# Routed experts on one core: a full-rate one-hot scatter with gates per slot, a reordered expert tail, and TensorE's pair loop written out

## The reference, cut to what matters

```python
logits = h @ w_router                       # 256 x 8
top_val, top_idx = lax.top_k(logits, 2)
top_w = softmax(top_val)
gates = sum(one_hot(top_idx, 8) * top_w)    # 256 x 8, two entries per token
for e in range(8):
    y = (silu(h @ w_gate[e]) * (h @ w_up[e])) @ w_down[e]   # 1024 -> 3584 -> 1024
    out = out + gates[:, e:e+1] * y
```

## Time and profile before

| | |
|---|---|
| median of 3 runs | 1938.88 us (1936.35 to 1943.38) |
| profiled execution, time / span | 1940.5 / 1938.8 us |
| PE, DVE, ACT, POOL busy, share of the span | 95%, 71%, 59%, 51% |
| mean granted clock of TensorE | 0.969 of full |
| bytes moved by DMA | 479.5 MB |

### The profile page before, as it was taken

One profiled execution on the slowest core, in us unless ns is written; L12 is line 12 of the kernel. 1 busy time (PEld: TensorE's weight loads), 2 busy tenths in 40 slices (PEclk: granted clock), 3 DMA queues, 4 the chain that ended last, 5 costly groups with the idle time before them and its releaser, 6 DMA issues.

```text
span 1938.8 us, 26811 instructions
## 1 busy us (share of the span) xinstructions
PE 1835.8 (95%) x9778; PEld 1564.0 (81%) x9778; DVE 1374.6 (71%) x1144; ACT 1142.2 (59%) x941; POOL 982.0 (51%) x476
## 2 busy tenths in 40 slices
PE   7979999998999998999989999999999899879999
PEld 6769998887787887887878878878788697769998
DVE  6455445454788887797878877988888776367775
ACT  6434444463676776766757767767677454535553
POOL 6030000101796976978959879789597214620000
PEclk9999999998999999999999999999999898689999
DMA  6445555532898997998989989989899433215551
GB/s 202 173 134 170 180 195 174 174 109 79 325 369 305 376 366 271 378 361 310 368 300 334 365 305 378 363 307 371 302 378 367 146 109 109 87 44 174 189 181 66
DMA packets 248535, 479.53 MB, mean 247 GB/s; under 512 B 15919, under 2 KB 84297, under 8 KB 248409
## 3 DMA queue, kind: packets, MB, share of 16 engines
q1 hardware_dynamic: 247545, 476.49, 69.8%
q10 hardware_dynamic: 864, 1.31, 0.2%
HBM read 476.72 MB, written 1.05 MB: 246 GB/s over the span
## 4 chain that ended last, share of the span: by engine, by line
PE 80%; DVE 9%; issue 5%; ACT 4%; POOL 1%; DVEq 0%; DMA 0%; SPq 0%; ACTq 0%; POOLq 0%
PE bank L1881 24%; PE bank L1883 23%; PE bank L1882 23%; DVE wl L1494 3%; PE bank L2177 2%; PE bank L2254 2%; ACT wh L1026 1%; PE bank L2207 1%; PE bank L1847 1%; DVE xT L1252 1%; DVE arena L1532 1%; PE bank L2315 0%; PE bank L1967 0%; DVE wl L438 0%; POOL wl L438 0%
## 5 line engine op out<-in xcount | busy, mean ns | idle before, releaser
L1881 PE MATMUL bank<-wh,xTh 128*128 128x512 f32 x1568 | 626.0, 399 | 29.9 <-DVE xTl L1577 8.4
L1883 PE MATMUL bank<-wh,xTl 128*128 128x512 f32 x1568 | 615.5, 393 | 0.0
L1882 PE MATMUL bank<-wl,xTh 128*128 128x512 f32 x1568 | 615.1, 392 | 0.0
L806 POOL TENSOR_TENSOR wl<-raw,wh 128x512 fp32r<-128x512 f32 x224 | 540.2, 2427 | 128.8 <-ACT wh L1026 111.9
L1494 DVE TENSOR_TENSOR wl<-raw,wh 128x1536 fp32r<-128x1536 f32 x224 | 489.6, 2205 | 78.4 <-ACT wh L1026 76.8
L1026 ACT ACTIVATE wh<-raw 128x2048 fp32r<-128x2048 f32 x224 | 429.3, 1918 | 138.8 <-PE bank L1883 138.8
L1881 PEld LDWEIGHTS bank<-wh,xTh 128*128 128x128 f32 x1568 | 297.3, 190 | 97.5 <-DVE wl L1494 19.2
L1883 PEld LDWEIGHTS bank<-wh,xTl 128*128 128x128 f32 x1568 | 297.0, 189 | 63.4
L1882 PEld LDWEIGHTS bank<-wl,xTh 128*128 128x128 f32 x1568 | 297.3, 190 | 60.9 <-issue 1.2
L806 POOL TENSOR_TENSOR wl<-arena,wh 128x512 fp32r<-128x512 f32 x112 | 301.9, 2710 | 77.7 <-ACT wh L1026 77.7
L438 DVE TENSOR_TENSOR wl<-raw,wh 128x2048 fp32r<-128x2048 f32 x110 | 254.8, 2332 | 74.3 <-ACT wh L431 72.5
(11 more groups left out here) (377 smaller groups left out, 1686.0 us busy)
## 6 DMA issues: line engine op xcount, KB each, us to landing
raw<-in_moe_w_up SPq DMA_DIRECT2D x112, 1024.0 KB, 5.8
arena<-in_moe_w_gate SPq DMA_DIRECT2D x96, 1024.0 KB, 5.4
raw<-in_moe_w_down SPq DMA_DIRECT2D x96, 1024.0 KB, 5.5
raw<-in_w_up SPq DMA_DIRECT2D x22, 1024.0 KB, 5.2
raw<-in_moe_w_gate SPq DMA_DIRECT2D x16, 1024.0 KB, 5.3
arena<-in_moe_w_down SPq DMA_DIRECT2D x16, 1024.0 KB, 6.0
raw<-in_gla_w_in SPq DMA_DIRECT2D x12, 1024.0 KB, 5.4
raw<-in_w_in SPq DMA_DIRECT2D x12, 1024.0 KB, 5.3
```

What stands on the lines that cost most here:

```text
L806: V.tensor_tensor(wl[:, s, LO_V:PIECE], moe_raw(c)[0][:, LO_V:PIECE], wh[:, s, LO_V:PIECE].bitcast(F32), ALU.subtract).then_inc(lo_moe[1], 1)
L1881: T.matmul(o, xh, yh, start=first, stop=False)
L1882: T.matmul(o, xh, yl, start=False, stop=False)
L1883: return T.matmul(o, xl, yh, start=False, stop=last)
```

## The change

1. `ohT` becomes an exact one-hot in fp32r (it lies over the idle `xT`), so `ohg` and its DVE operation go. The slot's gate is made by PE: two float32 matmuls of `oh` with a column of gates `gnow` into column 256 of bank 7, which DVE copies to `ghot`.
2. The eviction multiplies by that gate: ACT writes the high part `eyh` of each half, DVE the low part `eyl`. The scatter is then two fp32r passes for each of the four blocks, into banks 7, 4, 5 and 6 (before: 7 and 4 in turn, the third and fourth matmul behind an addition).
3. The tail: the transposes of j = 6 move between the two pieces of down(5), both gather halves run together, and the last down product goes half by half (`last_down`): each half is evicted by itself, and scattered once its low part is there. ACT's and DVE's orders follow; DVE now does the activation's low part and the product ahead of the weight piece in its turn.
4. DVE subtracts the whole 2048-column piece; POOL has no part in the experts; one semaphore in place of two.
5. PE's text: the first two pairs stand straight, a loop of `more + 1` passes and the last pair follow; PE reads the count after the second pair. The other engines keep `pairs`.

```diff
-LO_V = 1536
...
+with nc.sbuf_tensor("ohT", [P, S], F32R) as ohT:
+    pass
...
-lo_moe = [sg("lo_moe_v"), sg("lo_moe_p")]
+lo_moe = sg("lo_moe")
...
-    n = at(PC, c + 1)
-    for s in lo_moe:
-        eng.wait_ge(s, n)
+    eng.wait_ge(lo_moe, at(PC, c + 1))
...
-ohg = ar(TT * P).rearrange("p (t s) -> p t s", t=TT)
-ohT = ar(S)
+ghot, gnow = ar(1), ar(TT)
...
-ey = ar(D)
...
+eyh, eyl = (a.rearrange("p a n -> p (a n)") for a in (acth, actl))
...
-    def rests(at, more_follow):
-        for c in range(PC):
-            s = (M0 + c) % NW
-            pool.wait_ge(sg("hi_moe"), at(PC, c + 1))
-            V.tensor_tensor(wl[:, s, LO_V:PIECE], moe_raw(c)[0][:, LO_V:PIECE], wh[:, s, LO_V:PIECE].bitcast(F32),
-                            ALU.subtract).then_inc(lo_moe[1], 1)
-
-    pairs(pool, rests)
...
                     act.wait_ge(sg("moe_act"), at(2 * NEJ, n + 1))
                     V.activation(esg[:, n % 2, :], bank[n % 2][:, :], ACT.Silu).then_inc(sg("moe_silu"), 1)
                 tail = (kind, j, k) == ("d", NEJ - 2, 1)
-                if tail:
+                if kind == "g" and k == 1 and j >= 1:
+                    actT_hi(j - 1)
+                if (kind, j, k) == ("d", NEJ - 2, 0):
                     actT_hi(NEJ - 1)
-                if (kind, j, k) == ("d", NEJ - 1, 1):
-                    act.wait_ge(sg("moe_used"), at(PC, UC * (i + 1)))
-                    V.activation(ey[:, 0:512], bank[5][:, :], ACT.Copy).then_inc(sg("moe_y0"), 1)
+                if kind == "d" and j == NEJ - 1:
+                    if k == 0:
+                        act.wait_ge(sg("moe_yfull"), at(2, i + 1))
+                    else:
+                        act.wait_ge(sg("moe_used"), at(PC, UC * (i + 1)))
+                    act.wait_ge(sg("moe_ghot"), at(2, i + 1))
+                    V.activation(eyh[:, k * 512:(k + 1) * 512], bank[5 + k][:, :], ACT.Copy,
+                                 scale=ghot).then_inc(sg("moe_yh"), 1)
                 if c + NW < PC or more_follow:
                     moe_hi(at, c + NW)
                 else:
                     hi.upto(N_PRE + c + NW - PC)
-                if kind == "g" and k == 1:
-                    if j >= 1:
-                        actT_hi(j - 1)
-                    if j == 4:
-                        act.wait_ge(sg("moe_ohfull"), at(2, i + 1))
-                        V.activation(ohT, bank[7][:, 0:S], ACT.Copy).then_inc(sg("moe_ohT"), 1)
+                if (kind, j, k) == ("g", 4, 1):
+                    act.wait_ge(sg("moe_ohfull"), at(2, i + 1))
...
     more = pairs(act, experts, hi)
     for t in range(TT):
-        act.wait_ge(sg("moe_h"), more * 8 + (8 * NPAIR + 1 - 2 * (TT - 1 - t)))
...
         s = (M0 + c) % NW
         dve.wait_ge(sg("hi_moe"), at(PC, c + 1))
-        V.tensor_tensor(wl[:, s, 0:LO_V], moe_raw(c)[0][:, 0:LO_V], wh[:, s, 0:LO_V].bitcast(F32),
-                        ALU.subtract).then_inc(lo_moe[0], 1)
+        V.tensor_tensor(wl[:, s, :], moe_raw(c)[0], wh[:, s, :].bitcast(F32), ALU.subtract).then_inc(lo_moe, 1)
     def at_first(a, b):
         return b
...
         V.tensor_tensor(oh, iota2, pmu.unsqueeze(2).to_broadcast([P, TT, P]), ALU.is_equal).then_inc(sg("moe_oh"), 1)
         dve.wait_ge(sg("moe_oh"), value)
-    def onehot_gate(u, value):
-        gtu = gt[:, bass.ds(u, 1), :].rearrange("p a t -> p (a t)")
-        V.tensor_tensor(ohg, oh, gtu.unsqueeze(2).to_broadcast([P, TT, P]), ALU.mult).then_inc(sg("moe_oh"), 1)
-        dve.wait_ge(sg("moe_oh"), value)
+    def gates_now(u):
+        V.tensor_copy(gnow, gt[:, bass.ds(u, 1), :].rearrange("p a t -> p (a t)")).then_inc(sg("moe_gates"), 1)
     def gather_out(half, b, value):
...
+    gates_now(0)
     for c in range(2, NW):
         moe_lo_one(at_first, c)
...
             for q, (kind, j, k) in enumerate(uorder[:-2]):
-                tail = (kind, j, k) == ("d", NEJ - 2, 1)
-                if tail:
-                    gather_out(0, bank[7], at(4, 2 * i + 3))
-                    actT_lo(NEJ - 1)
-                    gather_out(1, bank[(NEJ * (i + 1)) % 2], at(4, 2 * i + 4))
-                weights_lo(q)
-                if not more_follow and UC * i + q + NW >= PC:
-                    lo.upto(N_PRE + UC * i + q + NW - PC)
-                if tail:
-                    for half in range(2):
-                        xg_lo(half, at(4, 2 * i + 3 + half))
                 if kind == "g" and k == 1 and j >= 1:
                     actT_lo(j - 1)
+                if (kind, j, k) == ("d", NEJ - 2, 0):
+                    actT_lo(NEJ - 1)
                 if kind == "u" and k == 1:
                     n = NEJ * i + j
                     dve.wait_ge(sg("moe_used"), at(PC, UC * i + q + 1))
...
                     V.tensor_tensor(eact[:, n % 2, :], esg[:, n % 2, :], bank[2 + n % 2][:, :],
                                     ALU.mult).then_inc(sg("moe_act"), 1)
-                    if j == 4:
-
-                        dve.wait_ge(sg("moe_ohfull"), at(2, i + 1))
-                        onehot(at(2, i + 1), at(4, 2 * i + 3))
-                        onehot_gate(at(2, i + 1), at(4, 2 * i + 4))
-            dve.wait_ge(sg("moe_used"), at(PC, UC * (i + 1)))
-            V.tensor_copy(ey[:, 512:1024], bank[6][:, :]).then_inc(sg("moe_y1"), 1)
+                weights_lo(q)
+                if not more_follow and UC * i + q + NW >= PC:
+                    lo.upto(N_PRE + UC * i + q + NW - PC)
+                if kind == "u" and k == 1 and j == 4:
+                    dve.wait_ge(sg("moe_ohfull"), at(2, i + 1))
+                    V.tensor_copy(ghot, bank[7][:, S:S + 1]).then_inc(sg("moe_ghot"), 1)
+                    gates_now(at(2, i + 1))
+                    onehot(at(2, i + 1), at(2, i + 2))
+                if (kind, j, k) == ("d", NEJ - 2, 1):
+                    for half in range(2):
+                        gather_out(half, bank[7] if half == 0 else bank[(NEJ * (i + 1)) % 2], at(4, 2 * i + 3 + half))
+                    for half in range(2):
+                        xg_lo(half, at(4, 2 * i + 3 + half))
+            for half in range(2):
+                hs = slice(half * 512, (half + 1) * 512)
+                dve.wait_ge(sg("moe_yh"), at(4, 2 * i + half + 1))
+                V.scalar_tensor_tensor(eyl[:, hs], bank[5 + half][:, :], ghot, eyh[:, hs].bitcast(F32),
+                                       ALU.mult, ALU.subtract).then_inc(sg("moe_yl"), 1)
             for q in range(4):
-                t, half = q // 2, q % 2
+                t, half = q % 2, q // 2
                 dve.wait_ge(sg("moe_scfull"), at(8, 4 * i + q + 1))
                 hs = h[:, t, half * 512:(half + 1) * 512]
-                V.tensor_tensor(hs, hs, bank[7 if q % 2 == 0 else 4][:, :], ALU.add).then_inc(sg("moe_h"), 1)
+                V.tensor_tensor(hs, hs, bank[(7, 4, 5, 6)[q]][:, :], ALU.add).then_inc(sg("moe_h"), 1)
             weights_lo(UC - 2)
             weights_lo(UC - 1)
...
     dve.wait_ge(sg("fg_in"), 16)
     for t in range(TT):
-        dve.wait_ge(sg("moe_h"), more * 8 + (8 * NPAIR + 1 - 2 * (TT - 1 - t)))
+        dve.wait_ge(sg("moe_h"), more * 8 + (8 * NPAIR + 1 - (TT - 1 - t)))
         C(V.tensor_tensor(xn[:, t, :], h[:, t, :], fgain, ALU.mult), "hg")
     def both_means(t):
...
                     ins = T.transpose(bank[4][:, k * P:(k + 1) * P], eact[:, n % 2, k * P:(k + 1) * P], ident[:, :])
                 ins.then_inc(sg("moe_Tfull"), 1)
-            def down(j):
+            def down(j, between=None):
                 n = NEJ * i + j
                 pe.wait_ge(sg("moe_actTl"), at(2 * NEJ, n + 1))
                 for part in range(2):
+                    if part and between is not None:
+                        between()
                     h_, l_ = here(UC * i + upos["d", j, part], 2)
                     for k in range(2):
                         kk = 4 * (n % 2) + 2 * part + k
                         for half in range(2):
                             hs = slice(half * 512, (half + 1) * 512)
                             ins = mm3(bank[5 + half][:, :], eactTh[:, kk, :], eactTl[:, kk, :], h_[:, k, hs], l_[:, k, hs],
-                                      j == 0 and part == 0 and k == 0, j == NEJ - 1 and part == 1 and k == 1)
+                                      j == 0 and part == 0 and k == 0, False)
                     used(ins)
+
+            def last_down():
+
+                n = NEJ * i + NEJ - 1
+                pe.wait_ge(sg("moe_actTl"), at(2 * NEJ, n + 1))
+                for half in range(2):
+                    hs = slice(half * 512, (half + 1) * 512)
+                    for part in range(2):
+                        h_, l_ = here(UC * i + upos["d", NEJ - 1, part], 2)
+                        for k in range(2):
+                            kk = 4 * (n % 2) + 2 * part + k
+                            ins = mm3(bank[5 + half][:, :], eactTh[:, kk, :], eactTl[:, kk, :], h_[:, k, hs], l_[:, k, hs],
```

(64 more changed lines are left out.)

## The result

The changed kernel takes 1907.46 us in the median of 4 runs (1905.59 to 1909.01), the kernel before 1938.73 on the same chip (4 runs, 1936.35 to 1943.38): a ratio of 0.9835, 95% interval 0.9814 to 0.9856, 31.3 us less. The profiled execution took 1909.0 (span 1907.3), 31.5 less than the one of before. The prediction was 1912 with 1902 to 1926.

A forecast was written before the change was run, and what follows sets the result against it. It took PE, busy 95% of the span, as the bound. Terms -10.9, -9.6, 0, -10.3 and +3.6 sum to -27.2 us, from the 1938.9 median to 1912 us; range 1902 to 1926 (forecast's own 1906 to 1919).

The forecast's parts named there:

- the forecast's own case: Whole kernel: the five parts together bring -27.2 us, giving 1912 us, own range 1906 to 1919; chance 0.56.
- Part 1: Ends of expert pairs: writing out PE's loop removes taken branches and a product wait, adds a count load; -10.9 us.
- Part 2: Once per expert: PE's stall before the fifth down product, waiting for the activation's low half, goes; -9.6 us.
- Part 3: Experts' weight pieces: DVE subtracts all 2048 columns at 2.29 us, covered by slack; price on PE's path 0.
- Part 4: Expert tail up to the next steady stream: new order saves 1.4 us for each of seven experts; -10.3 us in all.
- Part 5: Gates per slot: two added one-column fp32 matmuls on PE cost 0.45 us per expert; +3.6 us in all.
- (d): Steady expert cycle: DVE becomes the bound above 2.57 us per weight piece; 1950 us at 2.70; chance 0.04.
- the walk: Expert tail, timed step by step across PE, DVE and ACT: scatter ends 12.25 us after down(5), with one idle before.
- (a): Expert tail: DVE's queue is late for the next expert's weights; 1922 us, or 1929 with a further stall; chance 0.14.
- (b): Pair ends: the idle comes from other engines' loops, not PE's branch; only 0.9 gained there, total 1922; chance 0.07.
- (c): Expert tail covered better, by earlier ACT eviction or DVE: 1 to 1.5 us more per expert, 1901 to 1905; chance 0.10.
- (e): Steady expert stream: DMA becomes the bound, +5 to 8 us if cover fails at cycle ends, 1918 to 1920; chance 0.06.

The follow-up runs named there:

- the variant: PE's pair loop put back in the changed kernel, all else as changed: 1920.18 us, ratio 0.9886 to the kernel before.
- both edits of the last section: Changed kernel with ACT's second result eviction before its weight piece: 1902.53 us; also second-half scatter after next expert's first gate piece, DVE's additions later: 1899.68 us.

## Why the prediction was right, and where it was not

The total, the sign and the forecast's own case held. In the two profiled executions the terms are these:

| term | predicted | by the traces |
|---|---|---|
| Part 1, PE's loop | -10.9 | -11.2 = -10.65 (two excesses) - 0.9 + 0.36 |
| Part 2, stall before the fifth down | -9.6 | -10.5 = 8 x 1.31 |
| Part 3, DVE's whole piece | 0 | not apart from Part 2, see below |
| Part 4, tail | -10.3 | -13.2 = 7 x 1.71 and 1.2 |
| Part 5, gate matmuls | +3.6 | +3.4 = 8 x 0.42 |
| sum | -27.2 | -31.5 |

The terms of the traces add up to the whole by some luck: for the seven beats they give 28.5 of the 29.1 us that these lost, and 0.6 is spread over small steps that I did not assign.

**Part 1** held, in size and cause; two edits show it, one from each side. Of its small items the load of the count costs 0.36, not 0.7. The 0.9 for the product's wait is gone in the kernel after, as said, and not by the straight text: with the loop written out alone it stayed. With POOL out and the old order it was down to 0.3 a time; with POOL put back into the kernel after it stayed away. So the rest of the change is enough for it, and that it is the product's new place is the likely reading, not tried alone. That both branches cost the lower clock too, in the variant, is no general price: in the kernel before one restart kept the full clock and cost 3.5 us (4.44 less the 0.91).

**Parts 2 and 3: the step that failed** is Part 3's price of zero for DVE's taking over POOL's columns. That the stall goes under the new order fits the runs: with POOL put back and the rest of the change in place it stays away. But POOL's share was a cause of it as well: taken out of the kernel before alone, it removes the whole stall with the old order and both operations in place. Either of the two, POOL's leaving or the rest of the change, is enough, so the 10.5 us cannot be divided between them. And in the kernel after, the whole piece is not free: POOL put back costs 1.18 us an expert, 9.4 in eight, at another place, for DVE then is late with the product of the last block, whose transposes the change had moved forward. The prediction's walk was safe from this since it used d = 2.29 for all pieces, so the size came out right with Part 3's worth hidden in Parts 2 and 4. The number that should have warned stood in the earlier trace rows: four pieces in 10.08 us, 2.52 each, against the shortest of 1.75 in the earlier trace rows. I read this spread as a bound for rival (d) and not as a cost of the kernel before.

**Part 4**: the walk from the gathers to the new stream was right to 0.02 us. The 0.25 for late transposes did not occur; DVE pieces follow each other at 2.20 us though each lasts 2.29, which leaves DVE earlier than the walk had it:

```profile
592.27 2.29 DVE L1488 TENSOR_TENSOR wl<-raw,wh 128x2048 fp32r<-128x2048 f32 x1 [0.88 <-ACT wh L1016]
594.48 2.29 DVE L1488 TENSOR_TENSOR wl<-arena,wh 128x2048 fp32r<-128x2048 f32 x1
```

So the new tail is 12.23 + 0.44 = 12.67 against 14.38. The last expert gave 1.2, not 0.5: from its gathers to the transposes of the norm it takes 18.84 us, 0.44 for the moved transposes counted, where it took 20.07.

**Part 5**: 0.90 us from the first transpose to the stream, 0.45 before (0.42 more by the length of the whole cycle); the pace of the gather's weight loads was the right row.

```profile
549.36 0.38 PE L2258 MATMUL bank<-ident,arena 128*128 128x128 f32 x2
549.58 0.50 PE L2260 MATMUL bank<-arena 128*128 128x1 f32 x4
...
550.26 0.39 PE L1875 MATMUL bank<-wl,xTh 128*128 128x512 f32 x1
```

**Rivals.** (a), DVE late in the tail, did not come: no wait for a weight piece follows the scatter. (b) is refuted by the loop put back. (c) is not what the change does (ACT kept its order), but both edits of the last section make it so. (d) and (e) did not decide. Outside the experts two differences cancel: the first gather and the first matmuls of the profiled execution before lost some 3.3 us to the lower clock, which the one after did not, and the unchanged rest takes 412.6 us after against 409.0 before, at a mean clock of 0.91 against 0.92. I count neither for the change.

## What to carry to other kernels

The price of an instruction on one engine is its price beside its neighbours: before a stall is credited to an order of work, compare the shortest and the longest record of the same form, and see which engine runs beside the long ones. Take each suspect out alone, and put each back alone: here either of two steps removed the same stall, and one direction by itself would have named a single cause. A loop of PE with a long body costs the branch, 3.5 us a pass here, and 5.3 to 5.8 where the clock fell behind the idle; two passes of text written out took it away. Where the tail of one item leaves the bounding engine idle, move its last step behind the first piece of the next item: that made the fastest kernel here.

## What the runs showed that I had not expected

- Small DVE operations can suffer most beside POOL: 128 x 2 copied in 1.19 us against 0.16, 128 x 256 in 0.92 and 1.28 against 0.42, 128 x 1536 in 2.40 (mean) against 1.75 at least. It is not the operation as such: with POOL put back, the one-hot operation right behind that copy took 0.41.
- After 2.58 us idle the very first matmul was slow and eleven more ran at the lower clock. In the kernel before only the second of its two restarts fell to it, behind 3.03 us idle, and not the first, behind 3.06. What decides between them stays open.
- Waits in PE's straight text end 0.1 to 0.2 us sooner than in its loop and the pair behind it, where the values waited for are worked out in registers (0.84 against 1.04 us idle before the same down product, in one kernel). Why was not tried.
